# First norm by twos with unit transposes between, row 7's second norm ahead of S2's sums, down differences of two pairs moved: one streaming-encoder block on one core

## The reference

```python
def rms_norm(x, g):
    xf = x.astype(jnp.float32)
    y = xf * lax.rsqrt(jnp.mean(xf * xf, axis=-1, keepdims=True) + EPS)
    return (y * g.astype(jnp.float32)).astype(x.dtype)
...
        h = rms_norm(x, norm_mix_g[l])
        proj = jnp.einsum('bsd,de->bse', h, w_in[l])
...
        mix = jnp.concatenate([a_out, d_out], axis=-1)
        x = x + jnp.einsum('bse,ed->bsd', mix, w_out[l])
        h = rms_norm(x, norm_ffn_g[l])
        gate = jnp.einsum('bsd,df->bsf', h, w_gate[l])
        up = jnp.einsum('bsd,df->bsf', h, w_up[l])
        x = x + jnp.einsum('bsf,fd->bsd', jax.nn.silu(gate) * up, w_down[l])
```

## Time and profile before

| | |
|---|---|
| median of 3 runs | 1324.06 us (1323.51 to 1328.56) |
| profiled execution's own time | 1324.67 us |
| its span | 1322.9 us |
| TensorE busy | 1286.1 us (97%) |
| VectorE, ScalarE, GpSimd busy | 744.5, 580.6, 752.2 us |
| mean granted clock of TensorE | 0.994 |

### The profile page before, as it was taken

The page is one execution under the profiler, slowest core; times in us unless marked ns, Lnnn a source line. Parts: engine busy times, 40 slices in busy tenths (PEclk is TensorE's granted clock), DMA queues, the critical chain, the costliest instruction groups (busy, mean ns, idle before and its releaser), DMA issues.

```text
span 1322.9 us, 18379 instructions
## 1 busy us (share of the span) xinstructions
PE 1286.1 (97%) x6940; PEld 1071.6 (81%) x6940; DVE 744.5 (56%) x1033; ACT 580.6 (44%) x930; POOL 752.2 (57%) x516
## 2 busy tenths in 40 slices
PE   8999999999999989999988999999999999999999
PEld 7888888888878768888867878888888888788887
DVE  6455654535527667743588666565455556354552
ACT  5577645652136664552343322333333324454441
POOL 4332455642249992131168968988878784574541
PEclk9999999999999999999989999999999999999999
DMA  5611355521242005632211444433444337886663
GB/s 208 243 45 35 100 155 142 142 86 44 51 130 93 2 22 159 220 128 96 80 48 64 183 183 152 166 122 141 183 184 183 151 120 252 315 267 194 200 195 144
DMA packets 77807, 186.11 MB, mean 141 GB/s; under 512 B 20680, under 2 KB 24848, under 8 KB 70680
## 3 DMA queue, kind: packets, MB, share of 16 engines
q1 hardware_dynamic: 72144, 180.71, 40.3%
q10 hardware_dynamic: 5576, 4.23, 1.1%
HBM read 130.59 MB, written 56.94 MB: 142 GB/s over the span
## 4 chain that ended last, share of the span: by engine, by line
PE 73%; DVE 8%; POOL 6%; ACT 4%; DMA 4%; issue 3%; SPq 1%; DVEq 0%; ACTq 0%; POOLq 0%
PE ps L2007 21%; PE ps L340 20%; PE ps L2032 13%; PE ps L353 6%; POOL SX L843 3%; DMA RAWD<-w_down 2%; PE ps L1839 2%; PE ps L1871 1%; PE ps L1931 1%; PE ps L1854 1%; PE ps L325 1%; PE ps L1820 1%; DMA RAB<-down_t 1%; DMA RAB<-w_down 1%; POOL WR L742 1%
## 5 line engine op out<-in xcount | busy, mean ns | idle before, releaser
L340 PE MATMUL ps<-HT,SPLIT 128*128 128x512 f32 (+1 forms) x1488 | 329.9, 379 | 0.4 <-POOL SPLIT L290 0.4
L340 PEld LDWEIGHTS ps<-HT,SPLIT 128*128 128x128 f32 x1488 | 265.8, 190 | 50.1 <-issue 0.5
L2032 PE MATMUL ps<-S,HI 128*128 128x512 f32 x616 | 191.2, 392 | 2.0 <-POOL S L887 1.9
L887 POOL TENSOR_TENSOR S<-RAB,S 128x512 fp32r<-128x512 f32 x77 | 108.1, 1408 | 96.1 <-ACT S L1058 95.8
L288 POOL CAST SPLIT<-RAW 128x1024 fp32r<-128x1024 f32 x31 | 33.5, 1080 | 186.7 <-PE ps L340 181.8
L2032 PEld LDWEIGHTS ps<-S,HI 128*128 128x128 f32 x616 | 116.2, 189 | 27.0 <-issue 2.3
L2007 PE MATMUL ps<-HI,WR 128*128 128x512 f32 x368 | 119.9, 396 | 5.5 <-ACT UV L1023 5.4
L1540 DVE TENSOR_TENSOR LO<-RAB,HI 128x512 fp32r<-128x512 f32 x77 | 67.8, 892 | 93.9 <-ACT HI L1055 93.9
L2032 PE MATMUL ps<-S,LO 128*128 128x512 f32 x308 | 120.4, 391 | 0.0
L2007 PE MATMUL ps<-S,WR 128*128 128x512 f32 x504 | 117.8, 389 | 0.0
L2007 PE MATMUL ps<-HI,WX 128*128 128x512 f32 x336 | 110.4, 390 | 2.3 <-ACT UV L1023 1.5
(11 more groups left out here) (265 smaller groups left out, 2491.4 us busy)
## 6 DMA issues: line engine op xcount, KB each, us to landing
hidden<-HB SPq DMA_DIRECT2D x11, 1792.0 KB, 6.6
RAB<-hidden SPq DMA_DIRECT2D x77, 256.0 KB, 3.2
RAW<-units SPq DMA_DIRECT2D x37, 512.0 KB, 4.1
RAWG<-w_gate SPq DMA_DIRECT2D x11, 1024.0 KB, 10.8
RAWU<-w_up SPq DMA_DIRECT2D x11, 1024.0 KB, 4.8
RAWD<-w_down SPq DMA_DIRECT2D x11, 1024.0 KB, 8.8
down_t<-RAWD SPq DMA_DIRECT2D x11, 1024.0 KB, 3.9
RAB<-down_t SPq DMA_DIRECT2D x44, 256.0 KB, 3.9
```

What stands on the lines that cost most here:

```text
L340: mm = pe.matmul(ps[:, bank + a // HALF, a % HALF:a % HALF + width], w, right[other][:, k, a:a + width], start=(k == order[0] and part == ...
L887: pool.tensor_tensor(down_b(q, 1), RAB[:, q % RAWS, 1, :], down_b(q, 0).bitcast(F32), ALU.subtract).then_inc(R["b_lo"], 1)
L2032: mm = pe.matmul(ps[:, bank + t, :], down_a(q, part)[:, t * P:(t + 1) * P], down_b(q, other), start=(p == 0 and i in (1, 6, 5, 7) and part ...
```

## The change

Four edits. In the first norm ScalarE and VectorE go through rows 0 to 3 two at a time, then 4 to 7 in a mixed order, and TensorE turns rows 0 and 1, then the unit matrix 16 times, and from then on two rows after each slot 0 quarter. In the second norm VectorE adds and norms row 7 before S2's sums of span "0", which go behind row 7's quarter sums; ScalarE takes row 6's copies and one cast before row 7's norm; cast 4 waits for seven rows' transposes instead of eight. ScalarE's later casts and high parts move accordingly. The down differences of pairs 1 and 2 (counted from 0) move later, to gate product 6 and up product 2 of pair 2, and the queue issues pair 3's gate load before pair 1's `down_t` store and pair 3's up load before pair 2's.

```diff
-WARM = 48
+WARM, WARM_NEXT = 48, 16
...
+        INP_NORM_ACT = [("stats", 0), ("stats", 1), ("hi", 0), ("hi", 1), ("stats", 2), ("stats", 3), ("hi", 2), ("hi", 3),
+                        ("stats", 4), ("stats", 5), ("hi", 4), ("stats", 6), ("hi", 5), ("stats", 7), ("hi", 6), ("hi", 7)]
+        INP_NORM_DVE = [("scale", 0), ("scale", 1), ("lo", 0), ("lo", 1), ("scale", 2), ("scale", 3), ("lo", 2), ("lo", 3),
+                        ("scale", 4), ("scale", 5), ("lo", 4), ("scale", 6), ("lo", 5), ("scale", 7), ("lo", 6), ("lo", 7)]
...
-                        ("s1", 5), ("cast", 1), ("cast", 2), ("cast", 3), ("stats", 7)]
+                        ("s1", 5), ("cast", 1), ("cast", 2), ("cast", 3), ("part", 6), ("cast", 4), ("stats", 7)]
...
-                        ("s32", "0"), ("add", 7), ("scale", 7), ("part", 6), ("s1", 6)]
+                        ("s3", "0"), ("add", 7), ("part", 6), ("scale", 7), ("s1", 6), ("s3", "6")]
...
                         hidden_store(0)
-                    if 1 < p < NPF - 1:
+                    elif p == 1:
+                        hidden_store(1)
+                        raw_gate(3)
+                    elif p == 2:
+                        raw_up(3)
+                    elif p < NPF - 1:
                         raw_gate(p + 1)
                     sp.wait_ge(F["down_t"], 4 * (p + 1))
                     sp.dma_start(down_t[p], RAWD[:, :, :]).then_inc(F["raw_d_free"], 16)
-                    if 1 < p < NPF - 1:
+                    if 2 < p < NPF - 1:
                         raw_up(p + 1)
...
-                    if p:
+                    if p > 1:
                         hidden_store(p)
...
-                    act.wait_ge(nrm["ffn"]["turned"], NT)
+                    act.wait_ge(nrm["ffn"]["turned"], NT - 1 if n == 4 else NT)
...
                 s_lo_dve(dve, 0, "0")
                 part_dve(dve, 7)
-                s3_dve(dve, "6")
+                s2_dve(dve, "0")
                 s1_dve(dve, 7)
                 s3_dve(dve, "7")
...
-                    if n == PLACE[1, UP, 2]:
+                    if n == PLACE[2, GATE, 6]:
                         down_sums(dve, 1)
-                    if PRODUCTS[n][0] > 1 and PRODUCTS[n][1:] == (GATE, 2):
+                    if n == PLACE[2, UP, 2]:
+                        down_sums(dve, 2)
+                    if PRODUCTS[n][0] > 2 and PRODUCTS[n][1:] == (GATE, 2):
                         down_sums(dve, PRODUCTS[n][0])
...
-                for m in range(3):
+                for m in range(2):
                     norm_turn(pe, "inp", XN, m, 0)
+                for i in range(WARM_NEXT):
+                    pe.transpose(ps[:, 7, 0:P], ident[:, :], ident[:, :])
...
-                        m = 3 + 2 * quarter + slot
-                        if m < NT:
-                            norm_turn(pe, "inp", XN, m, 0)
+                        if quarter < 3 and slot == 0:
+                            for m in (2 * quarter + 2, 2 * quarter + 3):
+                                norm_turn(pe, "inp", XN, m, 0)
```

More of the change, by code:

```diff
@@ L119 @@
 S_DVE = {name: n + 1 for n, name in enumerate((
[2 rows of a table removed]
[2 rows of a table added]
     "s2half_1", "s2_1", "s2lo_1", "s4half_0", "s4_0", "s4half_1", "s4_1", "s4lo_0", "s4lo_1"))}
 S_ACT = {name: n + 1 for n, name in enumerate((
-    "s1_4", "s1_5", "s1_6", "s3_0", "s2_0", "s1_7", "s3_6", "s3_7", "s2_1", "s4_0", "s4_1"))}
+    "s1_4", "s1_5", "s1_6", "s3_0", "s1_7", "s3_6", "s3_7", "s2_0", "s2_1", "s4_0", "s4_1"))}
 U_SUM, X11, MID, V_SUM, X22, X12, X21 = 0, 4, 8, 20, 24, 28, 32
@@ L1079, in _ @@
                 act.activation(row_sum[:, 0:1], eps_col[:, :], ACT.Sqrt)
-                for m in range(NT):
-                    act.wait_ge(x_in[m], 16)
-                    norm_stats(act, "inp", XIN[:, m, :], JUNK, m)
-                    if m:
-                        norm_hi(act, "inp", m - 1, (HT[:, 0, :, :], HT[:, 1, :, :]), 0)
-                norm_hi(act, "inp", NT - 1, (HT[:, 0, :, :], HT[:, 1, :, :]), 0)
+                for step, m in INP_NORM_ACT:
+                    if step == "stats":
+                        act.wait_ge(x_in[m], 16)
+                        norm_stats(act, "inp", XIN[:, m, :], JUNK, m)
+                    else:
+                        norm_hi(act, "inp", m, (HT[:, 0, :, :], HT[:, 1, :, :]), 0)
                 act.wait_ge(ext_filled, 1)
@@ L1210, in _ @@
                 product_act(act, 0)
-                part_act(act, 6)
                 s1_act(act, 6)
                 s_act(act, 0, "0")
-                s_act(act, 1, "0")
                 part_act(act, 7)
-                weight_cast(act, 4)
+                weight_cast(act, 5)
                 product_act(act, 2)
                 s1_act(act, 7)
-                weight_cast(act, 5)
+                weight_cast(act, 6)
+                s_act(act, 0, "6")
                 product_act(act, 1)
-                s_act(act, 0, "6")
-                for n in (6, 7):
-                    weight_cast(act, n)
+                weight_cast(act, 7)
                 s_act(act, 0, "7")
+                s_act(act, 1, "0")
                 product_act(act, 4)
@@ L1574, in _ @@
                 dve.wait_ge(gain_mix_in, 16)
-                for m in range(NT + 1):
-                    if m < NT:
+                for step, m in INP_NORM_DVE:
+                    if step == "scale":
                         norm_scale(dve, "inp", XIN[:, m, :], gain_mix_bc, XN, m)
-                    if m:
-                        norm_lo(dve, "inp", m - 1, (HT[:, 0, :, :], HT[:, 1, :, :]), 0)
+                    else:
+                        norm_lo(dve, "inp", m, (HT[:, 0, :, :], HT[:, 1, :, :]), 0)
                 dve.wait_ge(small_in, 9 * 16)
@@ L1703, in _ @@
                         s1_dve(dve, t)
-                    elif step == "s32":
+                    elif step == "s3":
                         s3_dve(dve, t)
-                        s2_dve(dve, t)
                 s_lo_dve(dve, 0, "0")
                 part_dve(dve, 7)
-                s3_dve(dve, "6")
+                s2_dve(dve, "0")
                 s1_dve(dve, 7)
```

## The result

The changed kernel takes 1314.99 us (median of 5 runs, 1312.09 to 1315.51); five runs of the kernel before on the same chip took 1324.06 in the median. The ratio is 0.9911, 95% interval 0.9896 to 0.9926: 9.07 us off by the medians, where 5.0 were forecast. The profiled execution took 1314.99 us with a span of 1313.2, against 1322.9 before.

What follows compares the result with a forecast made beforehand. TensorE, fully busy in the hidden layer's long middle, was taken as the bound, with gains only where it idles. Terms -0.5 + 3.7 + 1.8 = 5.0 off 1322.9 gave 1317.9, as a median 1319.0 us; range 1315.3 to 1322.3.

Steps and rivals of the forecast that it cites:

- first norm: First norm, rows taken two at a time: 0.5 us slower, bounds 1.2 faster to 3 slower.
- start of the hidden layer: Second norm to thirteenth product: second product at 672.0, seventh 3.7 us earlier, thirteenth too; bounds 1.9 and 8.2.
- down differences: Third pair: TensorE's waits of 1.5 and 0.3 us go, 1.8 us gained.
- the scaling held by the split: First norm: row 2's scaling on VectorE waits out GpSimd's split, ending near 16.6; row 2 scaled at 17.9.
- an end within the bounds: First norm: the last quarter ends at 45.4 to 46.5; wrong if the end moved by over 2 us.
- the slow clock charged there: Pause before the fifth product: TensorE idle 2.9 us, so the clock falls, charged at 1.8 us.
- its slow clock unchanged: Thirteenth product: starts 3.7 us earlier, with the same slow clock as before.
- A pause over about 1.9 us costs 1.5 to 2.4 us more: TensorE's pauses anywhere: one over about 1.9 us brings slow clock, 1.5 to 2.4 us beyond its own length.
- The first rival: Fourth pair: the third pair's stall only moves there, the down edit gains 0, 1320.8 us; chance 0.2.
- Pauses of the first norm bringing slow clock: First norm: its pauses (0.4 and 0.8 close together, and 1.7) lose 1.5 to 2.5 us, 1321; chance 0.13.
- Pause before the fifth product closed: Start of hidden layer: VectorE meets GpSimd less, pause under 1.9 us or none, 1314.5 to 1317.3 us; chance 0.22.
- Slower: Start of hidden layer: GpSimd holds VectorE, row 7's low part ends later than before, 1325.3 us; chance 0.03.

Runs made afterwards that it cites:

- the old order and no fill: Whole kernels with the first norm of before, without 18 unit transposes ahead of the third row's; the changed kernel so: 1319.24, 1317.01 and 1319.11 us.
- the cut kernels: Kernel before and changed kernel, each ended after the first norm and four units: old norm 69.15 to 73.08 us, new norm 70.71 to 70.73.

## Why the prediction was wrong, point by point

The sum was -0.5 (first norm) + 3.7 (start of the hidden layer) + 1.8 (down differences) = 5.0 us. Each edit alone gained 2.6, 6.8 and 3.8 us by medians, and the whole 9.07 in the first comparison.

- **First norm, forecast 0.5 us slower: wrong, and this is the largest miss.** The steps held in the new trace: a first quarter in 3.1 us, its start (15.38 against 14.5, with row 0's transposes at 10.83, 1.2 us later than the 9.60 of the kernel before), the scaling held by the split, an end within the bounds. One reading was wrong without harm: the 2.03 us of the old scaling are the cast's doing and not the split's. The step that failed is the price of the edit, read from one execution: the first norm's length was taken for all that the edit changes, and its 3.19 us pause for the same in every execution. Alone the edit gained 2.6 us, taken out again it cost 1.9 to 4.1 (1318.2 against 1315.0 us in the mean of 24 and 22 executions, 3.2).

  Of these 3.2 us 3.1 are slow clock (5.9 against 2.7). Where it is lost is shown in part: in the first norm the six whole traces with the old order and no fill have 1.7 us of it five times and 3.4 once, the nine with the new norm none; but the new norm's other waits take that back, since the third units start only 0.1 us apart in the mean. By the point where TensorE is ready for the second product the six traces stand at 673.87 and the nine at 673.25 in the mean, 0.6 us apart, each group spread over 3.4 to 5.6 us. The race, worth about 0.5 us by the estimate above, fits that and no more. In the cut kernels the medians differ by 1.0 only. What makes the other 2 to 3 us stays open; that the shift moves later falls of the clock, the rival named for the edit alone, fits its trace, and no run tests it.
- **Start of the hidden layer, forecast 3.7 us: right mechanism, size off, 6.5 in the trace and 6.8 by medians alone.** Second product after a pause of 0.90 us (0.9 forecast), fifth product behind row 7's low part: both as said. The 2.8 us more are 0.7 for a pause before the fifth product of 2.17 instead of 2.9 (VectorE's operations ran short more often than I chose), 1.6 because the slow clock charged there did not come (5.7 us for both products instead of 7.3), and 0.5 behind the seventh product. So the term that was mis-sized is the gain up to the thirteenth product: 3.7 forecast, 6.5 measured, more than half of the difference a charge for slow clock that this execution didn't meet. That the thirteenth product keeps "its slow clock unchanged" was no step to build on either: the clock falls there or not with the same pause. The changed kernel's window in its first trace is shown above with 1.00; in a later trace of the same kernel, behind 2.40 us:

```profile
712.00:716.00 4.00, 4.00 (x12) 3.10 (x12) 2.48 (x5) 1.64 (x3) 3.84 (x4) 0.57 0.00 0
```

- **"A pause over about 1.9 us costs 1.5 to 2.4 us more": wrong as a rule.** It was drawn from seven pauses of one trace. The bound is near where I put it, but above it the clock fell behind 31 of 51 pauses up to 2.86 us, and behind all 8 from 3.15, and a fall cost 1.7 us, 3.4 behind two of these eight. The Trainium skill, page "TensorE: Matmul & The Clock Gate", section "Part 1: The HAM clock gate", has the chip judge TensorE's activity on a schedule that doesn't start with the kernel; equal pauses with unlike outcomes agree with it. By shares instead of a rule, the forecast would have charged the fifth product 1.0 instead of 1.8.
- **Down differences, forecast 1.8 us: right mechanism, a little small.** 2.3 us in the trace, 3.8 by medians alone with an interval from 0.8 to 5.3, 2.5 to 4.2 when taken out again. The waits counted were right (1.5 and 0.3 us, both gone); the 0.5 us beyond them, 0.2 at the short wait and 0.3 at the long one, weren't charged. The first rival, the stall moved to the fourth pair, is refuted: in the four traces of the whole TensorE has a wait there twice, of 0.42 and 0.46 us, and none in the other two.
- **The down stage's wait** wasn't a term at all. It fell from 1.95 to 0.48 us in the profiled pair, with its slow clock, 3.1 us of the 9.7 between the two spans; over 17 traces it runs from 0.3 to 2.9 with any code, so it explains this pair of traces and not the change. The delta rule's 3.85 us the other way hide it in the spans.
- **The rivals.** Pauses of the first norm bringing slow clock: no, none in nine traces of whole kernels and four cut executions. Pause before the fifth product closed: it was 2.1 to 2.2 us, above the rival's bound of 1.9, and kept the clock in 7 of the 11 traces that have it. So the result lies in that rival's 1314.5 to 1317.3, but not by its condition alone: a kept clock behind 2.17 us and a first norm worth more than forecast brought it there, which is luck for the rival. Slower: refuted.

## What to carry to other kernels

A profiled execution is one draw. Where TensorE's pauses lie near the length at which its clock falls, or an engine that others wait for races with another for the same memory access, look at the time and the granted clock of several executions before pricing an edit: here one trace priced the first norm's edit at 0.25 us lost, and 46 executions at 3.2 gained. A mechanism found in one long execution explains only as much as its frequency allows, so count it in the other traces before it is called the cause. A stretch that is cut out as a kernel of its own shows its spread cheaply. And where VectorE's chain sets a stretch's end, a wait removed at its front comes back at its end.

## What the runs showed that was not expected

- Unit transposes put into pauses do for the clock what they should and still don't pay: slow clock fell by 2.5 us in the kernel before, and the time did not.
- The order of the first norm's steps changed the spread of a stretch: the new norm's four cut executions agree within 0.02 us, the six of the old one differ by 3.9.
- The pause ahead of the delta rule's second step (about 552 us) took 1.12 to 2.60 us in code that is the same in all kernels, set by the landing of a load.
